# Attention as one run of 32 units, with its ropes, token-major values and key norms made inside the input projection

## The reference, cut to what matters

```python
pl = hl @ lp['w_in']                    # latent tokens; the context tokens the same way (pc)
ql, kl, vl = _split(pl[..., :ATT_IN_WIDTH], ATT_SPLITS)     # 8 query heads, 2 key and 2 value heads of 64
ql = rope_2d(ql.reshape(B, S, ATT_HEADS, HEAD_DIM), row, col)
kl = rope_2d(kl.reshape(B, S, ATT_KV_HEADS, HEAD_DIM), row, col)
att_l = window_attention(ql, kl, vl, kc, vc, lp['sink'])    # |i-j| <= 128, all 256 context keys, a sink logit
# rwkv_features:
pr = pr + lp['mu'] * (shift_centred(pr) - pr)
kk = _heads(k * lp['kk'])
kk = kk / jnp.maximum(jnp.sqrt(jnp.sum(kk * kk, axis=-1, keepdims=True)), 1e-12)
```

## Time and profile before

| | us |
|---|---|
| median of three runs | 1819.11 (1814.81 to 1820.21) |
| the profiled execution | 1817.26, of which the trace spans 1815.1 |
| input projection, from the first to the last matmul of its stage | 65.96 to 207.65 |
| value and key norm stage, from its first work to its last | 213.8 to 226.4 |
| attention, two passes, from their first work to their last | 228.6 to 294.3, 296.6 to 362.4 |
| the RWKV stage's first work | 366.4 |
| mean granted TensorE clock over the span | 0.942 of full speed |

### The profile page before, as it was taken

The page is one execution under the profiler, slowest core; times in us unless marked ns, Lnnn a source line. Parts: engine busy times, 40 slices in busy tenths (PEclk is TensorE's granted clock), DMA queues, the critical chain, the costliest instruction groups (busy, mean ns, idle before and its releaser), DMA issues. The chain is left out here.

```text
span 1815.1 us, 35800 instructions
## 1 busy us (share of the span) xinstructions
PE 1626.5 (90%) x15516; PEld 1324.2 (73%) x15516; DVE 743.0 (41%) x1108; ACT 577.3 (32%) x825; POOL 872.0 (48%) x431
## 2 busy tenths in 40 slices
PE   4899798958788887699999999999998899999996
PEld 2688566747676876477888888888876678888885
DVE  1312366766686763653111112550084521212134
ACT  3423333545343331424222323132221331323230
POOL 1433100168959560524888788833442344444441
PEclk9999999969999997898999999959998799999997
DMA  7311000003213131122444333311221112222221
GB/s 315 135 70 69 23 1 1 0 30 114 96 50 121 53 115 55 47 70 93 140 151 150 139 139 139 139 47 70 92 93 70 47 70 103 106 93 92 92 92 46
DMA packets 23450, 161.91 MB, mean 89 GB/s; under 512 B 2592, under 2 KB 3232, under 8 KB 4640
## 3 DMA queue, kind: packets, MB, share of 16 engines
q1 hardware_dynamic: 21744, 153.96, 23.9%
q10 hardware_dynamic: 1584, 6.13, 0.9%
HBM read 157.98 MB, written 2.10 MB: 88 GB/s over the span
## 5 line engine op out<-in xcount | busy, mean ns | idle before, releaser
L223 POOL TENSOR_TENSOR v<-raw,v 128x1024 fp32r<-128x1024 f32 x160 | 387.8, 2446 | 426.9 <-ACT v L211 400.7
L240 PE MATMUL bank<-hm,v 128*128 128x512 f32 x2112 | 487.5, 392 | 11.1 <-DVE hm L1863 4.9
L240 PEld LDWEIGHTS bank<-hm,v 128*128 128x128 f32 x2112 | 398.5, 189 | 100.1 <-issue 12.6
L240 PE MATMUL bank<-hid,v 128*128 128x512 f32 x1536 | 349.5, 389 | 0.0
L240 PEld LDWEIGHTS bank<-hid,v 128*128 128x128 f32 x1536 | 288.3, 188 | 59.9
L211 ACT ACTIVATE v<-raw 128x2048 fp32r<-128x2048 f32 x77 | 147.5, 1916 | 421.0 <-PE bank L240 420.9
L1989 DVE TENSOR_TENSOR bank<-bank,rl 128x512 f32<-128x512 f32 x64 | 44.8, 700 | 277.4 <-ACT rl L1968 277.4
L240 PE MATMUL bank<-h,w 128*128 128x512 f32 x744 | 141.7, 354 | 4.0 <-PEq L166 4.0
L240 PEld LDWEIGHTS bank<-h,w 128*128 128x128 f32 x744 | 120.9, 190 | 24.8 <-POOL w L223 4.4
L223 POOL TENSOR_TENSOR w<-raw,w 128x1024 fp32r<-128x1024 f32 x22 | 52.7, 2419 | 123.5 <-ACT w L211 123.5
L949 POOL TENSOR_TENSOR raw<-raw,cs 128x2048 f32<-128x2048 f32 x24 | 88.5, 3687 | 42.6 <-DVE at L1394 42.6
(11 more groups left out here) (292 smaller groups left out, 2361.8 us busy)
## 6 DMA issues: line engine op xcount, KB each, us to landing
raw<-w_in SPq DMA_DIRECT2D x119, 1024.0 KB, 4.8
mraw<-wm_in SPq DMA_DIRECT2D x16, 1024.0 KB, 4.7
raw<-wm_in SPq DMA_DIRECT2D x3, 1024.0 KB, 16.4
xres<-x_in ACTq DMA_DIRECT2D x1, 2048.0 KB, 9.6
yb<-wm_in SPq DMA_DIRECT2D x2, 1024.0 KB, 20.0
mixed_in<-wm_in SPq DMA_DIRECT2D x2, 1024.0 KB, 23.4
xres<-x_in SPq DMA_DIRECT2D x1, 2048.0 KB, 8.1
out_T<-xres ACTq DMA_DIRECT2D x8, 256.0 KB, 2.0
```

Of the source, the lines that this page charges most:

```text
L223: i = nc.gpsimd.tensor_tensor(W[1][n % 2][:, k:k + 4], raw[n % 2][:, k:k + 4], W[0][n % 2][:, k:k + 4].bitcast(F32), SUB)
L240: last = nc.tensor.matmul(bank(b(s, m), 0, hi - lo), W[w][s][:, k, m * P:(m + 1) * P], H[h][:, k, lo:hi], start=(k == 0 and w == h == 0), ...
```

## The change

In the input projection:

- From block 4 on, the tiles use two accumulators, `psum[0]` and `psum[1]`, and a tile waits for the evacuation of the same tile of the block before. `psum[2]` and `psum[3]` are free from there. PE's loop of three turns is written out.
- After block 2 (`Q_AT`) PE rotates the four query tiles with `rot`, and DVE ropes them in place. After block 5 (`K_AT`) it does so for the keys, and makes the six value transposes, copied out by ACT. SP copies the roped keys with their two heads swapped (`key_swap`), after its last weight load.
- The key norms: ACT squares `kk * k` (two tiles after block 6, two after block 7); PE sums each head over the partitions with the squares as weights and two columns, 24 matmuls after block 7 (`SUM_AT`); ACT takes one root and DVE one maximum and one reciprocal of 48 columns; PE spreads these over the partitions again after blocks 8 and 9 (`INV_AT`), 12 matmuls for each of four tiles, and DVE multiplies each tile into `kkT`.

Attention: the stage at L574, the two passes, the selection, the copies of values, the unused matmuls, the 32 reciprocals and POOL's products are gone. One stage runs 32 units in the same order as before, then 16 transposes and four copies. Tanh and sigmoid move from the end of ACT's projection program to the end of its attention program. The scratch lies in `x`, which is not read in between.

The diff, cut to its core:

```diff
-            t = psum[2 * (n % 2) + m]
+            t = psum[2 * (n % 2) + m if n < S_IN + 4 else m]
...
+                sp.wait_ge(roped, PAIRS + 1)
+                sp.wait_ge(tile_free[0][0], nth(S_IN + 4))
+                for lo, hi in ((0, HD), (HD, P)):
+                    sp.dma_start(key_swap[lo:hi], key_rot[P - hi:P - lo]).then_inc(swap_in, 16)
+                sp.wait_ge(swap_in, 32)
...
+                def in_turn(n, tiles, spans):
+                    s = n % 2
+                    pe.wait_ge(split_ready[s], nth(n))
+                    for m in range(tiles):
+                        pe.wait_ge(tile_free[(n - 1) % 2][m], nth(n - 1))
...
+                def spread(p):
+                    if p >= 2:
+                        pe.wait_ge(knormed, p - 1)
+                    for g in range(GD):
+                        for e in range(2):
+                            last = nc.tensor.matmul(psum[2 + p % 2][e * HD:(e + 1) * HD, g * P:(g + 1) * P],
+                                                    kinv[:, p * GD + g, e:e + 1].to_broadcast([P, HD]), K("ident"),
+                                                    start=True, stop=True)
+                    last.then_inc(kspread, 1)
...
+                    if n == Q_AT:
+                        pe.wait_ge(csa_in, 16)
+                        pe.wait_ge(tile_free[(S_IN + 1) % 2][1], nth(S_IN + 1))
+                        for i in range(PAIRS):
+                            nc.tensor.matmul(bank(2 * i + 1), KA("rot"), qT[:, i, :], start=True, stop=True)\
+                                .then_inc(rot_done, 1)
+                    if n == K_AT:
+                        pe.wait_ge(tile_free[0][1], nth(S_IN + 4))
+                        pe.wait_ge(tile_free[1][1], nth(S_IN + 3))
+                        pe.wait_ge(roped, PAIRS)
+                        nc.tensor.matmul(bank(4), KA("rot"), kvT[:, 0, C:N], start=True, stop=True).then_inc(rot_done, 1)
+                        for g in range(GD):
+                            last = nc.tensor.transpose(psum[3][:, g * P:(g + 1) * P], kvT[:, 1, g * P:(g + 1) * P],
+                                                       K("ident"))
+                        last.then_inc(vt_done, 1)
+                    if n == SUM_AT:
+                        for p in range(PAIRS):
+                            pe.wait_ge(ksq_ready, p + 1)
+                            for g in range(GD):
+                                at = 2 * (p * GD + g)
+                                last = nc.tensor.matmul(ksum[:, at:at + 2], kkT[:, p, g * P:(g + 1) * P],
+                                                        K("onesh")[:, ::HD], start=True, stop=True)
+                        last.then_inc(ksum_done, 1)
+                    if n in INV_AT:
+                        pe.wait_ge(kinv_ready, 1)
+                        for p in range(2):
+                            spread(2 * INV_AT.index(n) + p)
...
             def _(act):
                 for n in range(S_IN, S_MOD):
+                    if n == SUM_AT + 1:
+                        act.wait_ge(ksum_done, 1)
+                        nc.scalar.activation(kinv[:].rearrange("p g h -> p (g h)"), ksum, ACT.Sqrt).then_inc(kroot_ready, 1)
...
                     if n + 2 < S_MOD:
                         act_hi(act, n + 2, W)
+                    if n == K_AT:
+                        act.wait_ge(vt_done, 1)
+                        nc.scalar.activation(vtok.rearrange("p g c -> p (g c)"), psum[3][:, 0:N], ACT.Copy)
+                    if n in (S_IN + 6, SUM_AT):
+                        for p in (0, 1) if n < SUM_AT else (2, 3):
+                            act.wait_ge(mixed, 5 + p)
+                            nc.scalar.activation(kkT[:, p, :], kT[:, p, :], ACT.Square, scale=R("kk", p, p + 1))\
+                                .then_inc(ksq_ready, 1)
...
+                        if n == SUM_AT:
+                            flat = kinv[:].rearrange("p g h -> p (g h)")
+                            dve.wait_ge(kroot_ready, 1)
+                            link(nc.vector.tensor_scalar(flat, flat, 1e-12, None, MAX))
+                            nc.vector.reciprocal(flat, flat).then_inc(kinv_ready, 1)
+                        if n in INV_AT:
+                            for p in range(2 * INV_AT.index(n), 2 * INV_AT.index(n) + 2):
+                                dve.wait_ge(kspread, p + 1)
+                                nc.vector.scalar_tensor_tensor(kkT[:, p, :], kT[:, p, :], R("kk", p, p + 1),
+                                                               psum[2 + p % 2][:, 0:N], MUL, MUL).then_inc(knormed, 1)
...
+        units = [(i, b, h) for i in range(PAIRS) for b in range(NQ) for h in range(2)]
...
-                    keep_warm(6, bank(6))
...
-                    keep_warm(4, bank(6))
...
-                        if u in (1, 2):
-                            keep_warm(2, bank(7))
...
-                        s = nrm_flat[:, bass.ds(kv * (NU * SLICE) + u * SLICE, SLICE)]
-                        nc.vector.reciprocal(s, s).then_inc(inv_ready, 1)
```

More of the change, by code:

```diff
@@ L39, in _constants @@
     out["rot"] = rot
[L40 to L44, removed]
     m = 16
@@ L482, in _ @@
             def _(sp):
[L483 removed]
+                sp.dma_start(csa[:], A["csa"]).then_inc(csa_in, 16)
                 for i in range(PAIRS):
@@ L496, in _ @@
[L496 to L500, removed]
+                def in_turn(n, tiles, spans):
[3 more added lines that the diff above has]
+                        pe.wait_ge(tile_free[(n - 1) % 2][m], nth(n - 1))
+                        for k in range(KT):
+                            for w, e in ((0, 0), (0, 1), (1, 0)):
+                                for lo, hi in spans:
+                                    last = nc.tensor.matmul(acc(n, m, lo, hi), W[w][s][:, k, m * P:(m + 1) * P],
+                                                            hT[e][:, k, lo:hi], start=k == w == e == 0,
+                                                            stop=(k == KT - 1 and w == 1))
+                        last.then_inc(tile_done[s][m], 1)
@@ new lines, in _ @@
+                for n in range(S_IN + 1, S_MOD):
+                    if n < S_IN + 4:
+                        pe_block(pe, n, W, hT, parts=both[:1])
+                    elif n < S_MOD - 1:
+                        if n == S_IN + 4:
+                            pe.wait_ge(roped, 2)
+                        in_turn(n, 2, ((C, N), (0, C)))
+                    else:
+                        in_turn(n, 1, ((C, N),))
+                    if n == Q_AT:
[25 more added lines that the diff above has]
+                            spread(2 * INV_AT.index(n) + p)
@@ L523, in _ @@
                             for lo, hi in segs:
-                                i = nc.scalar.activation(d[:, lo - first:hi - first], acc(n, m, lo, hi), ACT.Copy)
+                                o = key_rot[:, lo:hi] if t == 8 and lo < C else d[:, lo - first:hi - first]
+                                i = nc.scalar.activation(o, acc(n, m, lo, hi), ACT.Copy)
                         else:
@@ L570, in _ @@
                     i.then_inc(mixed, 1)
-    proj.close()
[L574 to L616, removed]
@@ new lines, in _ @@
+                    if m or j == 14:
+                        if n == Q_AT:
+                            for q in range(PAIRS):
+                                dve.wait_ge(rot_done, q + 1)
+                                rope(qT[:, q, :], bank(2 * q + 1), qT[:, q, :])
+                        if n == K_AT:
+                            dve.wait_ge(rot_done, PAIRS + 1)
+                            rope(kvT[:, 0, C:N], bank(4), key_rot[:, C:N])
+                        if n == SUM_AT:
[8 more added lines that the diff above has]
+                                                               psum[2 + p % 2][:, 0:N], MUL, MUL).then_inc(knormed, 1)
```

345 lines of the change are left out of this document (150 added, 195 removed).

## The result

The changed kernel takes 1864.8 us (median of four runs, 1858.19 to 1865.15), the kernel before 1819.66 us. The ratio is 1.0222, with a 95% interval of 1.0151 to 1.0293: 45 us slower, where 35 us less were forecast. The trace spans 1862.4 us where it spanned 1815.1.

The account below looks back on a forecast made before the run. PE was taken as the bound, DVE close behind. 1.3 + 18.1 + 2.26 + 1.45 + 94.2 + 3 = 120.3 us replace 154.8, 34.5 less than 1817.26; with one us added, 1784 us, range 1774 to 1793.

Parts of the forecast that it names:

- The stretch up to the first `scores`: Projection and stage change before attention: last projection matmul near 228 us, first `scores` near 232 us.
- the first rival: Spreading after blocks 8 and 9 doesn't overlap in the array: 5.7 us more, 1790 us; chance 0.12.
- the fifth rival: Projection work stalls PE through the evacuation, 12 tiles of 2 us: 24 us more, 1808 us; chance 0.03.
- The unit's distance and its bound: Attention units: PE is the bound, eight units take 22.3 us, and losing the reciprocal gives nothing.
- the third rival: DVE, not PE, bounds the attention units: each shortens by up to 0.47 us, 1770 us; chance 0.10.
- part 4, the clock in the fill: At the attention's start the clock falls to 1.2 GHz and comes back: 2 us (0 to 4).
- the fourth rival: Without unused matmuls the clock doesn't come back in the attention: up to 89 us more, 1873 us; chance 0.03.
- The change of stage ahead of the attention and the end: PE idles 2.26 + 1.45 = 3.7 us before the first `scores`; after the last copy everything is as before.
- From there everything as before: Behind the attention's last copy, forecast near 328 us, the kernel's remainder was to be unchanged.
- The range: Whole kernel: 1774 to 1793 us, leaving out the last two rivals and far parts of the third's and clock's.

Follow-up runs that it names:

- the burst runs: The changed kernel with one burst of unused matmuls ahead of unit 16: 16 of 320 columns, ratio 1.0085; or 32 of 64 columns, 1.0347.
- the narrow burst: The changed kernel with one burst of 32 unused matmuls of 64 columns ahead of unit 16: 1883.37 us, ratio 1.0347 to the kernel before.

## Why the prediction was wrong, point by point

- **The stretch up to the first `scores` came out right, in part by luck.** Forecast near 232 us, measured 232.16. From its first to its last matmul the projection grew by 21.1 us (141.7 before, 65.83 to 228.62 after) where 18.1 and 1 for the clock were forecast. But it didn't start 1.3 us later: PE's idle time ahead of it went from 3.97 to 4.75 us, 0.8 more, and the work ahead of that ended 0.9 us sooner. The two errors nearly cancel. The spreading took 2.77 us for 24 matmuls, 5.5 us in all where 5.7 were forecast. That is 0.115 us each, and a quarter of the 0.875 us of a 512-column matmul would be 0.219 one after the other: two column groups do overlap in the array, as the Trainium skill, TensorEngine Tiling (Array Packing), Theoretical Speedup, says of 64 weight columns, and the first rival is out. Waits for the accumulators, ropes and PSUM didn't show: the fifth rival is out.
- **The head sums were mis-sized.** 7.2 us and 1 us for the clock were forecast; they took 9.8, and block 8 took 18.25, 1.0 more than the 17.21 of block 9. The idle of 1.92 us is there as worked out. What was missing is that the clock falls during the sums and is at 0.50 from 175 to 182 us, so that the second half of the sums takes 5.1 us in place of 2.6.
- **The unit's distance and its bound were right, at the clock of before.** 22.3 us for eight units was forecast if the clock is up, and the run with the unused matmuls back has 22.32. PE was the bound; without the reciprocals nothing got shorter: the third rival is out. (Its 0.47 us a unit should be 0.52 by its own working, 22.32 x 2.63 / 14.00, over 8.)
- **The failed step is part 4, the clock in the fill,** and with it the reasoning against the fourth rival. I took it that the clock would fall ahead of the attention and that the units, PE being busy without a gap, would lift it within some microseconds, 2 us in all. From the first `scores` to the last copy are 171.7 us, where 94.2 were forecast without the clock, so the clock cost 77.5 and not 2. The fall itself came later than I took it, among the first `scores`; what failed is the coming back. The row for the coming back, 300 to 302 us, is one of selection matmuls of 256 columns (L711) and not of units. The proof that I gave, 1.00 over 256 to 270 us with no unused matmul in it, shows only that a clock that is up stays up. It doesn't show that these units can lift one that is down, and the changed kernel and the burst runs show them not doing it, over 160 us. The mechanism of the fourth rival was right, with its place. Its price of 89 us was near: a unit takes 5.24 us at the low clock, 1.88 times as long and not twice, and 32 x 2.45 are 78. Its chance of 0.03 was far too small.
- **The rule of the Trainium skill,** TensorE: Matmul & The Clock Gate, What's actually happening, was weighed at 2 us. Its first half agrees with the runs: the slow clock is what PE falls back to (0.50 from 236 us on). Its second half, that activity lifts it, isn't borne out by PE being busy: 160 us of busy PE at 0.50, and the narrow burst. I read the rule as one on gaps.
- **The change of stage ahead of the attention and the end were right** to within some tenths of a microsecond: PE idles 3.55 us where 3.7 were forecast, and from the last copy to the RWKV stage's first matmul are 3.9 us (4.0 before). The one ahead of the projection cost 0.8 and not 1.3 us. "From there everything as before" was wrong by 6 us, and the cause is open.
- **The range** left this case out with intent. With the two outcomes 80 us apart and nothing in the trace that told which way the units would go, the slow one should have had a large share of the chances.

## What to carry to other kernels

Before you take out matmuls that nobody reads, or a dense stretch ahead of a run of small matmuls, look for a row in which work of that same kind lifts the clock; a row in which it keeps it is no substitute. Where filler is needed, put it into the wait at the start of the pipeline, right in front of the steady work: four matmuls there did what fourteen did, and six ahead of it didn't help. A saving that is planned as a shorter path through PE should be checked at both levels of the clock.

## What the runs showed of the hardware that was not expected

- PE busy 40.0 of 40.0 us in three windows in a row and 39.6 in a fourth, with the granted clock at 0.50 over these 160 us, and the same instructions at 1.00 behind one burst of 11 us.
- A burst of 14 us of 64-column matmuls left the clock at 0.50; the burst of 320-column ones was followed by 1.00.
- Head sums, 128x128 weights with two columns, lower the clock of the dense block behind them, whether or not PE waits among them. Behind 12 of them (2.6 us) the block took 18.3 to 18.4 us, behind 24 it took 18.2 to 19.5, against the 17.1 of block 9. Block 9 stands behind 24 spreading matmuls of 128 columns, 2.8 us, and the granted clock over 203 to 220 us is 1.00.
